# Sparse attention: the last nine selection rounds laid out over other units, and the first logits placed ahead of a wait

## The reference, cut to what matters

```python
score = jnp.einsum('bqh,bqhk->bqk', w_idx[:, start:end], jax.nn.relu(dots))
score = jnp.where(s_pos <= t_pos, score, -jnp.inf)
_, sel = lax.top_k(score, ktop)                  # ktop = min(256, S // 4) = 128
...
logits = (einsum(q, k_sel) * dh ** -0.5 + bias)  # then softmax, then p @ v_sel
```

## Time and profile before

| what | value |
|---|---|
| median of three runs | 805.03 us (803.84 to 806.48) |
| the profiled execution's own time | 806.08 us |
| its span in the trace | 804.0 us |
| granted TensorE clock, mean over the span | 0.983 of full |
| TensorE matmul busy | 748.3 us (93%) |
| VectorE busy | 615.0 us (76%) |
| ScalarE busy | 428.9 us (53%) |

### The profile page before, as it was taken

One profiled execution on the slowest core, in us unless ns is written; L12 is line 12 of the kernel. 1 busy time (PEld: TensorE's weight loads), 2 busy tenths in 40 slices (PEclk: granted clock), 3 DMA queues, 4 the chain that ended last, 5 costly groups with the idle time before them and its releaser, 6 DMA issues.

```text
span 804.0 us, 9843 instructions
## 1 busy us (share of the span) xinstructions
PE 748.3 (93%) x3555; PEld 566.1 (70%) x3555; DVE 615.0 (76%) x805; ACT 428.9 (53%) x512; POOL 109.7 (14%) x92
## 2 busy tenths in 40 slices
PE   3898999999999898999999998999999999999993
PEld 3666787776665555667888874788888887888782
DVE  5877786533999958653567658899999999999992
ACT  5434215256575443555423424776677777676760
POOL 4110000000010100002000011013233132413111
PEclk9999999999999998999999999999999999999997
DMA  9919996110130131105437336999999999999983
GB/s 286 373 35 408 373 359 214 53 52 1 53 106 0 53 105 53 37 18 185 157 104 283 137 158 215 414 402 374 381 387 386 386 387 385 387 385 381 379 285 56
DMA packets 86250, 184.78 MB, mean 230 GB/s; under 512 B 7024, under 2 KB 26584, under 8 KB 84160
## 3 DMA queue, kind: packets, MB, share of 16 engines
q1 hardware_dynamic: 78096, 156.02, 51.8%
q0 software_dynamic: 8112, 28.22, 12.2%
HBM read 171.48 MB, written 12.62 MB: 229 GB/s over the span
## 4 chain that ended last, share of the span: by engine, by line
PE 52%; DVE 29%; issue 7%; ACT 5%; DMA 5%; SPq 1%; DVEq 1%; POOL 0%; ACTq 0%; POOLq 0%
PE ps L672 14%; PE ps L674 13%; PE ps L673 13%; DVE w_lo L1976 8%; DVE accm L1676 3%; DVE score L1796 3%; DMA raw<-in_w_gate 3%; DVE m L1795 2%; DVE ys L2096 2%; ACT w_hi L1518 2%; PE ps L934 1%; DVE w_lo L1614 1%; PE ps L950 1%; DVE score L1782 1%; PE ps L962 1%
## 5 line engine op out<-in xcount | busy, mean ns | idle before, releaser
L1976 DVE TENSOR_TENSOR w_lo<-raw,w_hi 128x2048 fp32r<-128x2048 f32 x80 | 179.8, 2286 | 6.3 <-ACT w_hi L1518 6.3
L1518 ACT ACTIVATE w_hi<-raw 128x2048 fp32r<-128x2048 f32 x80 | 151.1, 1915 | 12.1 <-DMA raw<-in_w_gate 6.6
L672 PE MATMUL ps<-act_lo,w_hi 128*128 128x512 f32 x240 | 102.7, 428 | 6.6 <-DVE act_lo L1659 3.3
L672 PE MATMUL ps<-w_lo,hgT_hi 128*128 128x512 f32 x256 | 103.4, 404 | 5.0 <-DVE w_lo L1976 1.8
L674 PE MATMUL ps<-w_hi,hgT_hi 128*128 128x512 f32 x256 | 100.1, 391 | 0.0
L673 PE MATMUL ps<-w_hi,hgT_lo 128*128 128x512 f32 x256 | 100.0, 391 | 0.0
L674 PE MATMUL ps<-act_hi,w_hi 128*128 128x512 f32 x240 | 95.3, 397 | 0.0
L673 PE MATMUL ps<-act_hi,w_lo 128*128 128x512 f32 x240 | 94.9, 395 | 0.0
L1254 ACT ACTIVATE w_hi<-raw 128x2048 fp32r<-128x2048 f32 (+2 forms) x29 | 51.5, 1780 | 70.2 <-DMA raw<-in_w_in 47.1
L1614 DVE TENSOR_TENSOR w_lo<-raw,w_hi 128x2048 fp32r<-128x2048 f32 (+2 forms) x29 | 61.4, 2126 | 34.1 <-ACT w_hi L1254 33.9
L625 POOL DMA_INDIRECT out<-ys,slot_tok x15 | 48.8, 3256 | 160.4 <-DVE ys L2096 160.4
(11 more groups left out here) (284 smaller groups left out, 1328.4 us busy)
## 6 DMA issues: line engine op xcount, KB each, us to landing
raw<-in_w_down SPq DMA_DIRECT2D x32, 1024.0 KB, 15.8
raw<-in_w_gate SPq DMA_DIRECT2D x30, 1024.0 KB, 18.0
raw<-in_w_up SPq DMA_DIRECT2D x18, 1024.0 KB, 15.7
raw<-in_w_in SPq DMA_DIRECT2D x16, 1024.0 KB, 6.5
raw<-in_w_ada SPq DMA_DIRECT2D x16, 1024.0 KB, 7.7
raw_late<-in_w_up SPq DMA_DIRECT2D x14, 1024.0 KB, 19.0
raw<-in_w_ada SPq DMA_DIRECT2D x8, 512.0 KB, 7.0
raw_early<-in_w_ada SPq DMA_DIRECT2D x8, 512.0 KB, 6.8
```

What stands on the lines that cost most here:

```text
L672: pe.matmul(o, a[0], b[1], start=start, stop=False)
L1518: act.activation(e_hi[s_][:, :], e_raw[r][:, :], ACT.Copy).then_inc(e_top, 1)
L1976: dve.tensor_tensor(e_lo[s_][:, :], e_raw[r][:, :], e_hi[s_][:, :].bitcast(F32), ALU.subtract).then_inc(e_split, 1)
```

## The change

A table says how many rounds each unit of branch B does: one at p = 2 and 3, two at p = 4, 6 and 7, one at p = 8, none at p = 5. The last step of branch A (m = 15) does two rounds and not three. So 39 rounds are in branch A and 9 in branch B. Then `logits(0)` on TensorE waits for `a_ready` 15 alone (the step that had read `zt[0]`), and the wait for `a_ready` 16 comes after it. On VectorE `rows(0)` moves ahead of the waits for `a_ready` 16 and `oa_ps`.

```diff
         UNITS = [(i, hp) for i in range(NT) for hp in range(HP)]
+        ROUNDS_B = {2: 1, 3: 1, 4: 2, 6: 2, 7: 2, 8: 1}
...
+            pe.wait_ge(a_ready, len(STEPS) - 1)
+            logits(0)
             pe.wait_ge(a_ready, len(STEPS))
-            logits(0)
             logits(1)
             av_a(HP - 1)
             pe.wait_ge(side_sb, len(SIDE))
...
                 topk_rounds(2)
                 sums(m)
-                topk_rounds(2 if m < 8 else 1)
+                topk_rounds(2 if m < 8 else 1 if m < len(STEPS) - 1 else 0)
...
+            rows(0)
             dve.wait_ge(a_ready, len(STEPS))
             dve.wait_ge(oa_ps, HP)
-            rows(0)
             oa_low(HP - 1)
             for p in range(len(UNITS)):
                 if p + 1 < len(UNITS):
                     rows(p + 1)
                 normal(p)
                 gate_splits(FILL_A[-1] if p == 0 else FILL_B[p - 1])
-                topk_rounds(0 if p < 4 else 2)
+                topk_rounds(ROUNDS_B.get(p, 0))
                 if p >= 3 and p % 2:
                     ob_low((p - 3) // 2)
```

## The result

| | before | after |
|---|---|---|
| median (range, runs) | 805.31 us (803.84 to 806.48, 4) | 799.04 us (797.91 to 800.73, 4) |
| span of the profiled execution | 804.0 us | 797.3 us |
| ratio after / before | | 0.9925 (0.990 to 0.995) |

The change takes 6.3 us off the median; by the ratio it is 0.75%. The unchanged kernels were run again later, beside the experiments: 800.74 us against 804.55, which is 3.8 us by the medians and, by the ratio of 0.9941 (0.9921 to 0.9962), 4.7 us. The two intervals overlap from 0.9921 to 0.995, so the difference between the two sets can be noise.

A forecast was written before the change was run, and what follows sets the result against it. TensorE was taken to pace the units, except for a VectorE pause in unit 5 and the low clock behind it. 3.0 + 3.1 - 0.2 + 0.6 = 6.5 us off the 805.03 us median gave 798.5, range 796.0 to 801.8.

The forecast's parts named there:

- The bound: Units of branch B: TensorE paces them, except a 3.20 us pause before turn 6 made by VectorE in unit 5.
- Part 1: Unit 5 without its two rounds: turn 6 moves from 316.70 to 313.67, a 0.3 us pause stays; gain 3.0 us.
- Part 2: Turn 6 to turn 7: without the long pause the clock stays full, 5.71 us against 8.84; gain 3.1 us.
- Part 3: Rounds moved to other units: hidden in units 2, 3 and 8; turn 8 gives back 0.2 us.
- Part 4: Border of the branches: logits(0) runs beside ScalarE's last weights, and step 15's round must go too; gain 0.6 us.
- Part 5: Behind the units: nothing waits for a fixed moment, so the gain carries to the end in full.
- Rival 3: Experts' stream, DMA engines 98% busy, hides the gain: 805 us; chance 0.06.
- rival 2: VectorE paces the units once the clock is up, holding turns 7 and 8 about 1 us each: 800.5 us; chance 0.10.
- rival 4: Slower: rounds in units 2, 3 and 8 land on TensorE's path and the clock falls twice: 809.7 us; chance 0.02.
- Rival 1: The clock falls anyway or somewhere else, such as the router stage, costing 3.1 us: 801.6 us; chance 0.15.

The follow-up runs named there:

- e6: Kernel after, with the round of unit 8 done in unit 5 instead: 800.99 us, ratio 0.9946.
- e2: Kernel before with only the border changed (early logits(0), rows(0) ahead of the waits), rounds as before: 805.66 us, ratio 1.0005.
- e9: Kernel before once more, unchanged: 806.42 us (one run).
- e12: Kernel before with five extra row maxima on VectorE after the weight splits of units 1, 9 and 13: 821.69 us, beside 807.6 for before.
- e8: Kernel before with three matmuls of 512 columns filling TensorE's pause ahead of turn 6: 804.18 us, ratio 0.9987.
- e1: Kernel before with only branch B's rounds relaid (one at p = 2 and 3, two at 4, 6 and 7), border as before: 801.74 us, ratio 0.9949.
- e5: Kernel after, but step 15 keeps its third round and unit 8 has none: 800.62 us, ratio 0.9934.
- e3: Kernel before with the two rounds of unit 5 done in unit 8, nothing else: 800.11 us, ratio 0.9926.
- e7: Kernel after, with three more rounds moved from branch A (steps 12 to 14) to ahead of the splits of units 1, 5 and 9: 798.15 us, ratio 0.9900.
- e4: Kernel before with six matmuls of 512 columns put into TensorE's pause ahead of turn 6: 805.6 us, ratio 0.9997.

## Why the prediction was right, point by point

The forecast was 798.5 us in a range of 796.0 to 801.8, and 799.04 was measured. In the traces the 6.54 us of the stage are 0.55 up to turn 0, 3.05 up to turn 6, 2.89 up to turn 7 and 0.05 behind it; the forecast had 0.6, 3.0, 3.1 and -0.2.

**The bound.** TensorE paced by its own work, with one pause made by VectorE in unit 5: right in every row.

**Part 1, unit 5.** Forecast 3.0 us. From turn 0 to turn 6 the stage lost 3.05 (29.82 to 26.77), and the pause left over was 0.17 where 0.3 was said. The 313.35 at which I had TensorE free was 0.15 too early: by the row itself, a wait of 3.20 ahead of 316.70, it was free at 313.50. e6 puts one of the rounds back and gets 1.57 us of it back.

**Part 2, the clock.** Forecast 3.1, measured between these two traces 2.9 (turn 6 to turn 7, 8.68 to 5.79 in TensorE's timeline). I had ended the window of 8.84 us at 325.54, where the chain has turn 7; TensorE's timeline has it 0.16 earlier:

```profile
325.38 0.60 PE L950 MATMUL ps<-ident,lrow 128*128 128x128 f32 x4
```

The number is right and what it was taken for is not quite. I treated the low clock as what such a pause does. In four traces with this pause of 3.20 us (before, e2, e9, e12) it cost the unit 2.9, 1.5, 0 and 2.7 us. So the 3.1 was the upper end of what the pause can cost, and the profiled execution had drawn it. That the sum met the trace after is sound, since the forecast started from that very execution; that it also met the median within 0.6 us has luck in it. I named the reason as a rival and didn't use it for the size: by the Trainium skill ("TensorE: Matmul & The Clock Gate", Part 1) the activity window runs freely, and e2, e9 and e12 agree with that, in that one length of pause is followed by no fall, by a late one and by an early one. No run moved the phase by itself, so that it is the phase which decides stays argued.

The certain part of the change is the difference between e9, whose clock didn't fall, and after: 113.29 - 109.27 = 4.0 us, which are 3.0 in unit 5, 0.55 at the border and 0.5 at turn 8 (the mask). A fall adds less to the stage than to its unit, because turn 8, late already, then doesn't wait for the mask: 2.5 us in the first trace of before, 1.1 in e2 (114.21, and 0.2 for its border, against 113.29), 0 in e9, so 1.2 on average of three. e8 gives 1.0 (-0.3 to 2.5) by times. The change is thus worth about 5 us on average, an estimate from these traces; both ratios (0.9925 and 0.9941, 6.0 and 4.7 us) are in line with it within their intervals. Whether the two sets drew the fall unlike often can't be said, since only profiled executions show the clock of a stage.

**Part 3, the rounds elsewhere.** Units 2 and 3 hid theirs as forecast. For unit 8 the forecast gave back 0.2 at turn 8; there was no wait, VectorE turned from `normal(8)` to its next round at 323.19, 0.2 us ahead of turn 8 (323.39). My sum there was some tenths too long. What I had missed is why unit 8 has a round at all: if the last round is in unit 7, the mask write of 0.43 us goes with it, which is more than that 0.2, and turn 8 is 0.4 us late (e1, e5, e6, e8, e9), 0.5 by the end of the stage. In the first trace of before that was hidden by the low clock, and so no row showed it.

**Part 4, the border.** Forecast 0.6, measured 0.55 (21.07 to 20.52 at turn 0). "Without the removal the logits' gain would be lost there" was too strong: with the third round kept, turn 0 is at 20.86 (e2) and 20.87 (e5), so 0.2 of the 0.55 remain. The round's removal without the early logits was not run. By the rows it should bring next to nothing: in before `oa_low` starts at 285.08, 0.63 behind `oa_high` (284.45), and in after, where nothing but `oa_high` holds it, 0.73 behind. That is an estimate from rows and no measurement.

**Part 5, what carries.** All of it: 6.54 us in the stage, 6.7 in the span. Rival 3 (hidden by the experts' stream) is out, and so are rival 2 (turns 7, 8 and 9 wait for nothing in the kernel after) and rival 4. Rival 1 in its first form, a fall in spite of the short pause, was not seen in the eight traces whose longest wait of a turn was 1.7 us or less. In its second form, a fall elsewhere that grows, it is no matter of the change: the router's stretch at the low clock is as long in after as in before (mean clock 0.97 from 440 to 500 us in both), and in e9, the kernel before unchanged, it was longer (0.91).

**The range.** 6.5 + 0.35 + 0.5 and a spread of 1.4 on either side give 796.3 to 799.9 and not 796.0 to 800.5; the stated range went up to rival 1 in any case, so nothing hangs on it.

## What to carry to other kernels

Look for the unit in which the filling work and a rare large piece (here a weight split, every fourth unit) meet; moving two small pieces out of that one unit brought nearly all of the gain (e3, 109.86 against 109.27), and the room ahead of the large piece, while its input is still on the way, can be used too (e7). Ask also what comes with the last small piece: here it brings a mask write, and a unit that was just full was over by it. When a profile shows a stretch of low clock behind a pause, count the pause as certain and the clock as a range, since the trace shows one draw of it (here one and the same pause cost 0 to 2.9 us), and take a second trace of the unchanged kernel before crediting a change with it. With differences of 4 us ahead of the stage from one execution to the next, a ruler inside the trace resolves tenths where medians resolve two microseconds.

## What the runs showed of the hardware

Of seven unfilled pauses of TensorE between 3.1 and 3.5 us (before, e2, e9, and four in e12), six were followed by the 1.2 GHz level (granted clock 0.50) and one was not. The cost to the next unit was 0, 1.4, 1.5, 1.5, 2.7, 2.8 and 2.9 us. No pause of 1.7 us or less in front of a turn was followed by it (eight traces), nor the two that were filled with matmuls (e4, e8), though with one of the seven unfilled ones passing freely two are few. A filling matmul of 512 fp32 columns with the identity took about 0.9 us (six in 5.31, three in 2.73), against 0.23 for one pass of the fp32r products.
